# Sparse attention of a four-layer kernel: where the block compression and the compressed scores stand among the projections

## What is computed

```python
proj = h @ w_in
q = proj[..., :Q_COLS]            # 16 heads of 64
kv = proj[..., Q_COLS:...]        # six blocks of 4 groups x 64: compressed, selected, window (k and v each)
gates = sigmoid(proj[..., last 48] + b_gate)
# _compress: blocks of 32 tokens, one every 16 -> 15 blocks
blocks = blocks + pe
k_c = gelu(flat(blocks) @ w1, approximate=True) @ w2      # the same for v_c
# for each head
s_c = q * scale . k_c - slope * distance                  # 256 x 15 compressed scores
p_c = masked_softmax(s_c);  o_c = p_c @ v_c
# s_s, s_w: scores against the selected and the window keys, softmax, values
o = g0 * o_c + g1 * o_s + g2 * o_w
return o @ w_out
```

## Time and profile before

| | before |
|---|---|
| median of 3 runs | 1383.15 us (1383.14 to 1383.69) |
| span of the profiled execution | 1382.5 us |
| TensorE busy (matmuls) | 1346.9 us, 97% |
| TensorE weight loads busy | 1195.1 us, 86% |
| VectorE busy | 864.3 us, 63% |
| ScalarE busy | 673.8 us, 49% |
| GpSimd busy | 87.7 us, 6% |
| memory read and written | 212.41 and 1.06 MB, 154 GB/s over the span |
| TensorE from 323.84 us to 377.39 us | second query tile, gates, second compression layer, key tile |
| TensorE from 377.39 us to 424.70 us | attention |

### The profile page before, as it was taken

One profiled execution on the slowest core, in us unless ns is written; L12 is line 12 of the kernel. 1 busy time (PEld: TensorE's weight loads), 2 busy tenths in 40 slices (PEclk: granted clock), 3 DMA queues, 4 the chain that ended last, 5 costly groups with the idle time before them and its releaser, 6 DMA issues.

```text
span 1382.5 us, 26707 instructions
## 1 busy us (share of the span) xinstructions
PE 1346.9 (97%) x11635; PEld 1195.1 (86%) x11635; DVE 864.3 (63%) x1388; ACT 673.8 (49%) x1202; POOL 87.7 (6%) x104
## 2 busy tenths in 40 slices
PE   8999999999999999999999999999999998999997
PEld 6888998988867889998799999799987896799996
DVE  6786655573395655556685666856467556856565
ACT  6775544552384545442651224445443468545452
POOL 3000400000060000000000430000000000000000
PEclk9999999999999999999999999999999999999999
DMA  9345555453302555554233000655545451555550
GB/s 350 124 182 198 183 183 183 183 198 123 147 38 68 193 189 188 196 191 151 105 140 123 4 5 34 240 200 184 183 183 183 153 183 62 179 193 190 199 184 31
DMA packets 17635, 215.18 MB, mean 156 GB/s; under 512 B 1976, under 2 KB 2144, under 8 KB 4848
## 3 DMA queue, kind: packets, MB, share of 16 engines
q1 hardware_dynamic: 15888, 205.54, 40.3%
q0 software_dynamic: 1632, 7.94, 1.6%
HBM read 212.41 MB, written 1.06 MB: 154 GB/s over the span
## 4 chain that ended last, share of the span: by engine, by line
PE 84%; DVE 9%; ACT 4%; DMA 1%; issue 1%; SPq 0%; DVEq 0%; ACTq 0%
PE psum L665 24%; PE psum L471 11%; PE psum L472 11%; PE psum L473 11%; PE psum L1008 3%; DVE w_low L1862 3%; PE psum L1089 2%; PE psum L569 1%; PE psum L1141 1%; ACT w_high L1342 1%; PE psum L540 1%; PE psum L565 1%; PE psum L541 1%; PE psum L542 1%; DMA ring<-weights 1%; PE psum L561 1%
## 5 line engine op out<-in xcount | busy, mean ns | idle before, releaser
L1862 DVE TENSOR_TENSOR w_low<-ring,w_high 128x1024 fp32r<-128x1024 f32 x368 | 437.0, 1222 | 231.7 <-ACT w_high L1342 231.7
L1342 ACT ACTIVATE w_high<-ring 128x1024 fp32r<-128x1024 f32 x368 | 368.6, 1047 | 175.9 <-PE psum L665 155.4
L471 PE MATMUL psum<-act_split,w_high 128*128 128x256 f32 x1312 | 381.7, 291 | 3.7 <-DVE w_low L1862 3.6
L472 PE MATMUL psum<-act_split,w_high 128*128 128x256 f32 x1312 | 372.5, 284 | 0.0
L473 PE MATMUL psum<-act_split,w_low 128*128 128x256 f32 x1312 | 372.3, 284 | 0.0
L665 PE MATMUL psum<-w_high,up_split 128*128 128x512 f32 x1024 | 287.6, 391 | 0.8 <-DVE up_split L2010 0.8
L471 PEld LDWEIGHTS psum<-act_split,w_high 128*128 128x128 f32 x1312 | 252.6, 193 | 11.6 <-DVE w_low L1862 4.7
L472 PEld LDWEIGHTS psum<-act_split,w_high 128*128 128x128 f32 x1312 | 253.0, 193 | 2.6 <-issue 1.4
L473 PEld LDWEIGHTS psum<-act_split,w_low 128*128 128x128 f32 x1312 | 252.9, 193 | 0.0
L665 PEld LDWEIGHTS psum<-w_high,up_split 128*128 128x128 f32 x1024 | 190.4, 188 | 40.5 <-issue 2.7
L665 PE MATMUL psum<-w_low,up_split 128*128 128x512 f32 x512 | 163.1, 390 | 0.0
(11 more groups left out here) (338 smaller groups left out, 1661.3 us busy)
## 6 DMA issues: line engine op xcount, KB each, us to landing
ring<-weights SPq DMA_DIRECT2D x95, 2048.0 KB, 7.8
work<-rows POOLq DMA_DIRECT2D x4, 1024.0 KB, 5.0
ring<-weights SPq DMA_DIRECT2D x4, 512.0 KB, 8.5
work<-rows POOLq DMA_DIRECT2D x4, 512.0 KB, 5.6
x<-x_in SPq DMA_DIRECT2D x2, 512.0 KB, 4.4
work<-t_bias POOLq DMA_DIRECT2D x1, 1024.0 KB, 8.9
out<-x SPq DMA_DIRECT2D x4, 256.0 KB, 2.0
con<-consts SPq DMA_DIRECT2D x1, 687.0 KB, 21.6
```

What stands on the lines that cost most here:

```text
L471: mm(out, w_hi, x_hi, start=start, stop=False)
L472: mm(out, w_hi, x_lo, start=False, stop=False)
L1342: A(high[:, HIGH_SLOT[name], f], ring[:, n % RING, f], ACT.Copy).then_inc(weights_high, 1)
L1862: V.tensor_tensor(low[:, n % RING, f], ring[:, n % RING, f], high[:, HIGH_SLOT[name], f].bitcast(f32), ALU.subtract).then_inc(weights_spli ...
```

## The change

The block compression is no longer spread over the second query tile: all its 128 matmuls stand in one block between the two query tiles. The second query tile is projected in two halves, with `c_k` and `c_v` between them (`compressed_heads`), and the gate projection behind. In the key projection the gate transposes and all 32 compressed-score matmuls stand together behind step 6 (the seventh step). ScalarE does the GELUs before the split of `nsa_k`, and the exp of the compressed logits between the two halves of the split of `nsa_o0`. VectorE does `compressed_logits`, half of the split of `nsa_o0`, `compressed_probs`, and the other half, all ahead of the attention's loop. `nsa_w1` and `nsa_q1` change places in the order of the tiles, in memory and in the ring; turns and bank numbers follow the new order. No arithmetic is added or left out.

```diff
-    + ["nsa_v", "nsa_c", "nsa_q0", "nsa_q1", "nsa_w1", "nsa_k", "nsa_o0", "nsa_o1"] + _mlp_tiles(1)
+    + ["nsa_v", "nsa_c", "nsa_q0", "nsa_w1", "nsa_q1", "nsa_k", "nsa_o0", "nsa_o1"] + _mlp_tiles(1)
...
-for _n, _w in [("v", 2), ("c_in", 2), ("lam", 1), ("q", 4), ("c_hid", 1), ("gate", 1),
-               ("c_k", 1), ("c_v", 2), ("gate_t", 1), (("k", 0), 1), ("c_score", 2), (("k", 1), 1)]:
+for _n, _w in [("v", 2), ("c_in", 2), ("lam", 1), (("q", 0), 1), (("q", 1), 1), ("c_hid", 1), (("q", 2), 1),
+               ("c_k", 1), ("c_v", 2), (("q", 3), 1), ("gate", 1), ("gate_t", 1), ("c_score", 2), (("k", 0), 1),
+               (("k", 1), 1)]:
...
-            def compress(step):
-
-                for l in (2 * step % CMP_LEN, 2 * step % CMP_LEN + 1):
-                    kv = 2 * step // CMP_LEN
-                    if l == 0:
-                        pe.wait_ge(sig("c_blocks"), kv + 1)
+            for kv in range(2):
+                pe.wait_ge(sig("c_blocks"), kv + 1)
+                for l in range(CMP_LEN):
                     for hf in range(2):
                         last = mm(psum[half(hf), BANK[hid], kv * 32:kv * 32 + 2 * NCMP],
...
-            project("nsa_q1", TURN["q"] + 2, act_split, beside=lambda step: step < 31 and compress(step))
-            compress(31).then_inc(bank_filled, 1)
+            last.then_inc(bank_filled, 1)
...
+            project("nsa_q1", TURN[("q", 2)], act_split, ms=(0, 1))
+            compressed_heads()
+            project("nsa_q1", TURN[("q", 3)] - 1, act_split, ms=(2, 3))
...
-                if step == 0:
+                if step == 6:
                     q = TURN["gate_t"]
...
-                if step == 3:
                     for i in range(4):
-                        read_out(pe, TURN["q"] + i)
+                        read_out(pe, TURN[("q", i)])
                     read_out(pe, TURN["c_k"])
-                if 4 <= step < 31:
-
-                    for at in range((step - 4) * 16 // 27, (step - 3) * 16 // 27):
+                    for hf in range(2):
+                        open_bank(c_scores + hf)
+                    for at in range(16):
...
             queries(0)
             queries(1)
-            split("nsa_k")
-            queries(2)
-            queries(3)
             q = TURN["c_hid"]
             filled(q)
             A(c_hid[:, 0, :], bank(q)[:, 0:2 * NCMP], ACT.Gelu_apprx_tanh)
             taken(A(c_hid[:, 1, :], bank(q)[:, 32:32 + 2 * NCMP], ACT.Gelu_apprx_tanh), q)
+            split("nsa_k")
+            queries(2)
+            queries(3)
...
-            split("nsa_o0")
+            split("nsa_o0", [0, 1])
+            act.wait_ge(sig("c_logits"), 1)
+            done(A(c_s, c_s, ACT.Exp), "c_exp")
+            split("nsa_o0", [2, 3])
...
-            act.wait_ge(sig("c_logits"), 1)
-            done(A(c_s, c_s, ACT.Exp), "c_exp")
...
-            split("nsa_o0")
...
             compressed_logits()
+            split("nsa_o0", [0, 1])
+            compressed_probs()
+            split("nsa_o0", [2, 3])
             dve.wait_ge(sig("bias_done"), 16)
...
-                if j == 0:
-                    compressed_probs()
```

More of the change, by code:

```diff
@@ L791, in _ @@
                start=True, stop=True).then_inc(bank_filled, 1)
-            project("nsa_q0", TURN["q"], act_split)
+            project("nsa_q0", TURN[("q", 0)], act_split, second=TURN[("q", 1)])
             w_cmp = whole_tile("nsa_w1")
@@ L806, in compress, with compressed_heads @@
                                   c_blocks[half(hf), kv, l, :], start=(l == 0), stop=(l == CMP_LEN - 1))
-                return last
-            project("nsa_q1", TURN["q"] + 2, act_split, beside=lambda step: step < 31 and compress(step))
-            compress(31).then_inc(bank_filled, 1)
+            last.then_inc(bank_filled, 1)
+            def compressed_heads():
+                read_out(pe, TURN["c_hid"])
+                q = TURN["c_k"]
+                open_bank(q)
+                for hf in range(2):
+                    last = mm(psum[half(hf), BANK[q], 0:2 * NCMP], col("w2", 0, DH)[half(hf), :],
+                              c_hid[half(hf), 0, :], start=True, stop=True)
+                last.then_inc(bank_filled, 1)
+                for hf in range(2):
+                    q = TURN["c_v"] + hf
+                    open_bank(q)
+                    for c in range(2):
+                        for i in range(4):
+                            last = mm(psum[32 * i:32 * i + NCMP, BANK[q], c * DH:c * DH + DH],
+                                      c_hid[half(hf), 1, c * NCMP:(c + 1) * NCMP], col("w2", DH, DH)[half(hf), :],
+                                      start=True, stop=True)
+                    last.then_inc(bank_filled, 1)
+            project("nsa_q1", TURN[("q", 2)], act_split, ms=(0, 1))
+            compressed_heads()
+            project("nsa_q1", TURN[("q", 3)] - 1, act_split, ms=(2, 3))
             q = TURN["gate"]
@@ L820, in _ @@
             last.then_inc(bank_filled, 1)
[L822 to L837, removed]
             c_scores = TURN["c_score"]
-            for hf in range(2):
-                open_bank(c_scores + hf)
             def beside_keys(step):
-                if step == 0:
+                if step == 6:
                     q = TURN["gate_t"]
@@ L1570, in queries @@
             def queries(i):
[L1571 removed]
+                q = TURN[("q", i)]
                 filled(q)
@@ L2755, in _weights @@
     w1 = w1.transpose(2, 0, 1, 3).reshape(DH, TILE)
-    t += _tiles(w[:, :D][:, order])
-    t.append(np.concatenate([w1, w1], 0))
+    q0, q1 = _tiles(w[:, :D][:, order])
+    t += [q0, np.concatenate([w1, w1], 0), q1]
     t += _tiles(np.concatenate([kv[2], kv[4]], 1))
```

## The result

The changed kernel takes 1374.55 us (median of 4 runs, 1373.9 to 1375.04), the kernel before took 1383.42 in the same session: a ratio of 0.9937, 95% interval 0.9923 to 0.995. It is faster, by 8.9 us. The forecast was 1368.4 with a range up to 1373.8, so about 6 of the 15 us did not come, and the time lies just outside the range.

The account below looks back on a forecast made before the run. The prediction took TensorE to bound the kernel, with 84% of the chain that ended last. Gains of 9.4 (compression), 4.8 (scores) and 0.55 (attention entry) sum to 14.75 us, from 1383.15 to 1368.4 us; range 1366.3 to 1373.8.

Parts of the forecast that it names:

- The compression block: Between the query tiles: 256 issues in one block take 7.75 us with the visit, instead of 17.15; gain 9.4 us.
- the one that carried over: Compression block's pitch taken from the later RWKV mixer's recurrence: 256 issues in 7.44 us, 0.029 each.
- the 363.2 of the forecast: Sign: first attention score starts at 363.2 instead of 377.39; wrong if later by more than 1 us.
- The score block: Key projection: 64 issues at 0.055 us, with visit and transposes 3.95 us instead of 8.75; gain 4.8 us.
- the treatment of the clock: Both blocks: clock loss was argued against because the recurrence of the same form ran whole at granted clock 1.00.
- The clock rival: Both blocks and 6.5 us behind each run at 1.2 GHz, costing 17.4 us: 1385.8 us; chance 0.03.
- Short-group pitch: Rival: both blocks keep the pitch of short groups, gains 5.9 + 3.0 + 0.55 us: 1373.7 us; chance 0.11.
- Loads bind: Rival: in both blocks 64-column loads take 0.06 us, 128-column loads 0.12: 1380.6 us; chance 0.03.
- The moved heads and the waits: Heads between the second query tile's halves, and reordered loads and splits: all waits covered, 0 us.
- The entry of the attention: Early softmax removes the 2.73 us wait, but `factors(0)` then waits for ScalarE: gain 0.55 us, between 0 and 1.0.

Follow-up runs that it names:

- the held block: Also called the held kernel: the changed kernel with the load of `nsa_k` held until the compression block has ended; 1370.64 us, ratio 0.9908.
- the late one: Changed kernel, load of `nsa_k` held, scores in four groups, exp and probabilities of the compressed branch back where the kernel before has them; 1373.14 us, ratio 0.9923.
- compression alone: The changed kernel with the scores' part undone, so only the compression stands in one block; 1377.58 us, ratio 0.9962.
- eight groups: Changed kernel, load of `nsa_k` held, scores in 8 groups of 8 issues at steps 0 to 14, gate transposes at step 4; 1370.7 us, ratio 0.9902.
- groups of 32: Changed kernel, load of `nsa_k` held, scores in two groups: steps 6 and 10, 1369.93 us and again 1370.32; steps 0 and 9, 1368.01.
- groups of 16: Changed kernel, scores in four groups: load of `nsa_k` held, 1373.75 us; held with softmax late, 1373.14; not held, compression in 8 groups, 1371.2.
- 8 groups of 32: Changed kernel with compression in 8 groups of 32 issues in the first query tile, scores in 4 groups of 16, no load held; 1371.2 us, ratio 0.9923.

## Why the prediction missed

**The compression block.** Step by step the term was right: from the last plain product before it to the second behind it, less two plain pitches, the held block costs (331.31 - 323.29) - 0.24 = 7.78 us, against the forecast 7.75. The step that failed is the one that carried over: "The block's own pitch is not in this stage, but the recurrence of the later RWKV mixer has the same form". The recurrence has the same instructions, but no weights move there, 0.02 of DMA share. Here `nsa_k` moves, at a share of 0.84, a fact that stands in the prediction as an arrival ("the load of `nsa_k`, asked for at the end of the first query tile"). SyncE's queue was looked at for when data lands, and not for what it does to TensorE's instructions. A dense block of narrow matmuls uses a packet of instructions in a few us: in the held kernel the first came 2.8 us into the block and the next 3.8 later. The groups of 8 between large products did not need them so fast (330.7 and 340.6 in the kernel before), so that TensorE did not stop there. The sign could have been read all the same: that instruction packets mostly start late in a weight load stands in the trace of the kernel before, in its DMA queues. The price: stop 1.57 us; 38 issues in 2.34 instead of 1.10, 1.24 us more; some 17 products at 0.21 instead of 0.12, 1.6; and 0.2 on the first product. Together 4.6, the 4.66 that are missing. With the 1.6 of the scores, and less the 0.66 by which the stage began sooner, this is also the 5.6 us by which the first attention score (368.76) came later than the 363.2 of the forecast.

The Trainium skill, Runtime: NRT & Kernel Launch, section Instruction fetch mechanics, says that instructions are refilled in blocks of 16 KiB over a DMA queue of the sequencer, and that crossing from one to the next is mostly hidden. This case agrees on the packets (0.02 MB each) and on "hidden" for the recurrence alone; under a weight load the crossing cost 1.57, 1.66 and 1.97 us, and the measurement decides. The Trainium skill, DMA: Bandwidth & Descriptors, section Queues, rings and completion order, has each DMA engine take turns between its queues and empty a whole packet, typically some 9 to 17 descriptors, before it switches. The load's 144 packets in the profile are 9 for each of 16 engines. If those are the page's descriptors, a load is one such packet on each engine, and instructions that come mostly 5 us or more into it agree with the page. That they are the same no run here shows.

**The score block.** Right in size: 353.08 to 357.31 in the kernel after is 4.23, less 0.24 is 3.99, against 3.95. The failed step is the treatment of the clock: "Against it: the recurrence of the same form ran whole at 1.00". For the form 64*64 this held, 256 issues in 7.65 us at 1.00. It was used for the scores as well, whose form is 64*128 with 15 columns, and no row of before shows that form dense. The clock fell behind or inside the one block in 4 profiles of 4. In the changed kernel it cost 16 products at 0.21 instead of 0.12, 1.5 us: 4.8 - 1.5 = 3.3, measured 3.23.

**The clock rival** had the right mechanism for one half of it and 3% of the chance. It was priced for the case that both blocks and 6.5 us behind each ran at 1.2 GHz, 17.4 us. What came was 6.8 us (with the stop, so by the load and not by the block) and 3.4 us. That cost 1.24 + 1.6 + 0.2 and 1.5, so 4.5 us, a quarter of the price, and the kernel stayed faster. It lacked a case between the forecast and its own 1385.8. *Short-group pitch* would give 1373.7, near the result, but by the wrong cause: 5.9 + 3.0 was forecast for a pitch of 0.043, and the pitch was 0.030. *Loads bind* is excluded by the same row.

**The moved heads and the waits.** Right. ScalarE's split of `nsa_q1` ended at 323.06, well before its use at 333.71; the heads' visit (341.44) shows no idle before it, and neither does the gate or the key tile. Holding `nsa_k` back by 8 us, which was an experiment and no part of the change, used that cover: its split starts at 339.00 and ends at 342.9, before TensorE wants it at 346.26.

**The entry of the attention.** The moves came as described, but the gain is not certain. TensorE in the kernel after, and VectorE's `factors(0)`:

```profile
368.76 2.89 PE L873 MATMUL psum<-work 64*128 64x128 f32 x32 [0.94 <-ACT work L1594]
371.58 1.10 PE L886 MATMUL psum<-con,work 128*128 128x128 f32 x8
372.61 0.71 PE L873 MATMUL psum<-work 64*128 64x128 f32 x8
375.18 1.98 PE L873 MATMUL psum<-work 64*128 64x256 f32 x8 [1.86 <-DVE small L2198]
```

```profile
373.78 0.20 DVE L2210 RECIPROCAL small<-small 128x8 f32<-128x8 f32 x1 [1.88 <-ACT work L1607]
```

The wait of 2.73 us is gone, and `factors(0)` waits for ScalarE, both as foretold. TensorE then stands 1.86 us a little later, for VectorE, and is at half the clock behind it, as it was in the kernel before. With the early softmax the stage gained 0.45 and 0.44 in two profiles, lost 0.25 or 0.26 in five and lay between -0.51 and 0.21 in three; with the late one it was 0.01 and, for compression alone, -1.16. For the last the clock accounts: it was at 0.50 from 372.8 to 376.2, just when the first scores ran, which took 4.53 us instead of 2.89, so 1.64 more:

```profile
372.78 4.53 PE L877 MATMUL psum<-work 64*128 64x128 f32 x32 [0.94 <-ACT work L1595]
```

With the early softmax, where the clock falls seems to matter too: in the two profiles with the largest gain it fell 6.6 and 7.6 us behind the first score, in the five that lost 0.25 or 0.26 between 12.4 and 12.9 us behind it. But with eight groups it fell 7.2 us behind it and the stage lost 0.51, so the clock doesn't explain all. So the 0.55 of the forecast was seen in two profiles of ten and can't be told from 0 in the rest.

**What stays open** is why the clock keeps up in some kernels with score groups and not in others. One block fell in 4 profiles of 4, groups of 32 in none of 3 and of 8 in none of 1, groups of 16 in 2 of 3. The two pairs of equal programs each agreed in this stage (3.23 and 3.21, 4.42 and 4.42), so it may go by what the program does and not only by chance; but the same four groups at the same steps kept the clock in one kernel and lost it in two. The Trainium skill, TensorE: Matmul & The Clock Gate, part on the HAM clock gate, names idle gaps as what lowers the clock in mid-kernel. The fall behind the stop of 1.57 us, which went when the stop went, agrees in kind; the fall at the score block, with no idle ahead of it, does not. No run here varied the columns of these matmuls, so whether the fall goes with them wasn't tried.

## What to carry to other kernels

A row of dense matmuls is a safe price for another dense block only if the same transfers run beside both: look at what each DMA queue does during the new block, the instruction queue among them. The kernel before can tell: see how far into a load its instruction packets start, and how fast the new block will use them up. A bulk load beside a long run of short instructions can be moved by one wait in its queue, and here that was worth nearly half as much as the change (ratio 0.9908 against 0.9937). With it, and with the scores in two groups instead of one, the kernel took 1368.01 us against 1376.45 for the change in the same session, and 1384.29 before. When blocks of narrow matmuls are packed together, give the clock a rival of its own with a middle case, and give ratios from many executions, since one profile can be off by several us.

## What the chip showed beside that

A visit to another array form costs 0.30 us however many issues it has: 8 groups of 32 against one block cost 7 x 0.30 = 2.1 (45.71 against 43.63), and eight score groups against two cost 21.33 - 19.64 = 1.69, where 6 x 0.30 = 1.8. With sixty-four issues of 64*128 with 15 columns in one block, which keep TensorE 100% busy, the clock fell within or behind them in 4 profiles of 4; with 256 issues of 64*64 with 30 columns, about twice as long, and no load beside them, it did not fall in any of seven. Instruction packets mostly start late in a weight load: over all 14 profiles 375 start inside a single 2 MB load, two of them in its first 0.2 us and none of the others before 3.1 us. And an instruction packet that came late cost twice, first as a stop and then as a lowered clock that lasted 6.8 us.
